# Up-projection of a two-layer trunk on one core: ten panel pairs with a second level of block products instead of eight, and other places for the modulation panels

## The reference, cut to what matters

```python
D_MODEL = 1024; D_FF = 2816; N_MOD = 9
def swiglu(u, w_up, w_down):
    h = u @ w_up                       # 1024 x 5632
    a, b = jnp.split(h, 2, axis=-1)
    return (jax.nn.silu(a) * b) @ w_down

def trunk_layer(l, x, c, ...):
    mod = (jax.nn.silu(c) @ P['ada_w'][l] + P['ada_b'][l]).reshape(B, N_MOD, D)
    sh1, sc1, g1, sh2, sc2, g2, sh3, sc3, g3 = [mod[:, i][:, None, :] for i in range(N_MOD)]
    u = rmsnorm(x, ng[0]) * (1.0 + sc1) + sh1
    x = x + 0.5 * g1 * swiglu(u, P['w_ffn_up'][l, 0], P['w_ffn_down'][l, 0])
    ...                                # token mixing
    u = rmsnorm(x, ng[2]) * (1.0 + sc3) + sh3
    x = x + 0.5 * g3 * swiglu(u, P['w_ffn_up'][l, 1], P['w_ffn_down'][l, 1])
```

## Time and profile before

| | |
|---|---|
| median of three runs | 3149.52 us (3148.24 to 3153.7) |
| the profiled execution | 3147.8 us, span 3146.1 us |
| PE busy | 3096.7 us of the span (98%) |
| DVE, POOL, ACT busy | 1267.5, 1175.2, 417.9 us |
| chain that ended last | PE 95%, DVE 2%, DMA 2%, ACT 1% |
| DMA | 337.64 MB, mean 107 GB/s |
| side panels (ws<-w_ada) | 64 of 1024 KB, median 4.8 us from issue to landing |

### The profile page before, as it was taken

The page is one execution under the profiler, slowest core; times in us unless marked ns, Lnnn a source line. Parts: engine busy times, 40 slices in busy tenths (PEclk is TensorE's granted clock), DMA queues, the critical chain, the costliest instruction groups (busy, mean ns, idle before and its releaser), DMA issues.

```text
span 3146.1 us, 45962 instructions
## 1 busy us (share of the span) xinstructions
PE 3096.7 (98%) x18874; PEld 2502.2 (80%) x18874; DVE 1267.5 (40%) x2645; ACT 417.9 (13%) x806; POOL 1175.2 (37%) x1181
## 2 busy tenths in 40 slices
PE   7999999999999999999999999999999999999999
PEld 5778887678777878888877788876777778788887
DVE  3334532454233464445243344234533234644432
ACT  2000001212111120000011000023021111210000
POOL 4755431210000338764366644302100003487542
PEclk9999999999999999999999999999999999999999
DMA  6564223441111224322225532234311113122221
GB/s 247 196 241 151 86 76 107 155 145 40 52 51 51 85 81 155 114 92 76 86 100 224 217 137 83 80 116 148 125 56 42 44 59 104 67 93 82 85 80 66
DMA packets 73520, 337.64 MB, mean 107 GB/s; under 512 B 10592, under 2 KB 27744, under 8 KB 40288
## 3 DMA queue, kind: packets, MB, share of 16 engines
q1 hardware_dynamic: 63936, 312.03, 27.8%
q0 software_dynamic: 6816, 18.88, 2.0%
q10 hardware_dynamic: 2560, 3.80, 0.3%
HBM read 326.55 MB, written 6.02 MB: 106 GB/s over the span
## 4 chain that ended last, share of the span: by engine, by line
PE 95%; DVE 2%; DMA 2%; ACT 1%; issue 0%; SPq 0%; DVEq 0%; ACTq 0%
PE ps L830 94%; DMA ws<-w_ada 1%; DVE ws L1987 1%; DVE u L1987 0%; DMA lp<-params 0%; ACT ws L1692 0%; DMA ring<-w_ada 0%; ACT u L1692 0%; DVE proj L1987 0%; PE ps L897 0%; DVE masked_room L2415 0%; DVE x L1990 0%; PE ps L1519 0%; DVE masked_room L1987 0%; DVE y L1987 0%
## 5 line engine op out<-in xcount | busy, mean ns | idle before, releaser
L830 PE MATMUL ps<-u,ring 128*128 128x272 f32 x5120 | 1259.7, 397 | 11.5 <-ACT u L1692 9.3
L830 PEld LDWEIGHTS ps<-u,ring 128*128 128x128 f32 x5120 | 950.2, 190 | 231.0 <-issue 27.1
L1987 DVE TENSOR_TENSOR ws<-ws,ps 128x272 f32<-128x272 f32 (+5 forms) x1258 | 497.1, 413 | 1347.2 <-PE ps L830 1331.2
L724 POOL TENSOR_TENSOR masked_room<-ring 128x512 f32<-128x512 f32 (+1 forms) x44 | 55.6, 1265 | 986.7 <-DVE pause L2741 653.3
L1692 ACT ACTIVATE ws<-ps 128x272 f32<-128x272 f32 (+1 forms) x398 | 154.6, 396 | 1260.1 <-PE ps L830 1260.0
L830 PE MATMUL ps<-y,ring 128*128 128x272 f32 (+1 forms) x1376 | 296.7, 353 | 0.0
L830 PE MATMUL ps<-y,ws 128*128 128x272 f32 (+1 forms) x1296 | 296.7, 370 | 0.0
L830 PEld LDWEIGHTS ps<-y,ring 128*128 128x128 f32 x1376 | 230.8, 190 | 50.5 <-issue 10.3
L830 PEld LDWEIGHTS ps<-y,ws 128*128 128x128 f32 x1296 | 227.2, 190 | 35.8
L830 PE MATMUL ps<-proj,ring 128*128 128x272 f32 (+1 forms) x1088 | 240.4, 366 | 1.5 <-DVE proj L1987 1.5
L1692 ACT ACTIVATE ws<-ws 128x272 f32<-128x272 f32 (+4 forms) x170 | 105.8, 633 | 868.7 <-DVE ws L1987 817.2
(11 more groups left out here) (219 smaller groups left out, 3037.2 us busy)
## 6 DMA issues: line engine op xcount, KB each, us to landing
ring<-w_up SPq DMA_DIRECT2D x88, 1024.0 KB, 4.8
ws<-w_ada SPq DMA_DIRECT2D x64, 1024.0 KB, 4.8
ring<-w_down SPq DMA_DIRECT2D x32, 1024.0 KB, 4.8
ring<-w_gate SPq DMA_DIRECT2D x32, 1024.0 KB, 4.8
ring<-w_in SPq DMA_DIRECT2D x22, 1024.0 KB, 4.8
ws<-cache SPq DMA_DIRECT2D x128, 128.0 KB, 3.1
ws<-cache POOLq DMA_DIRECT2D x128, 128.0 KB, 3.4
ring<-w_down SPq DMA_DIRECT2D x16, 768.0 KB, 4.1
```

The costliest lines, as they stand in the source:

```text
L724: nc.gpsimd.tensor_tensor(sums[:, 0], a21, a22, ALU.add).then_inc(w_sums.sem, 1)
L830: return nc.tensor.matmul(out, lhsT, rhs, start=start, stop=stop, skip_group_check=skip)
L1987: return V.tensor_tensor(out, a, b, op)
```

## The change

- `PAIRS` goes from 8 to 10. Panels 2 to 21 are ten pairs, panels 0 and 1 stay single, and the four single panels at the end are gone, with their sums on POOL, additions on DVE and activations on ACT.
- The rooms of the inner token sums move, since `proj` tiles 16 to 19 are now needed for hidden tiles of pairs 8 and 9 while the sums are still read: they lie in `proj` 20 and 21, in the free half of `u`, in a new tile `last_inner`, and one of each four is formed in place in `tsum`.
- The 16 first hidden sums stand elsewhere on DVE: four in pair 8, three in pair 9, eight in pair 10, each time after `c22_b` and before step 4, and the last one after pair 10. They get other rooms (`HID_ROOM`).
- The down-projection's first two sums on POOL wait for pair 10 instead of single panels.
- The modulation panels stand elsewhere within a pair: panel 0 after M2a (before: after M1b), panel 1 after M5a (before: after M2b), panel 2 after the front of 4 (before: after M5b), panel 3 at the pair's end (before: ahead of M3b).

```diff
-PAIRS = 8
+PAIRS = 10
 SINGLE = FT - 2 * PAIRS
...
+HID_ROOM = (8, 9, 10, 11, 12, 13, 14, 4, 5, 6, 7, 0, 1, 2, 3)
...
-        inner_tok = proj[:, 16:22, :].rearrange("p a (b n) -> p (a b) n", n=HALF)
+        last_inner = sb("last_inner", [P, HALF])
...
+        def inner_tok(t, i):
+
+            if i == 2:
+                return tsum[:, t, 0:2, QUARTER:HALF]
+            n = 3 * (t - 1) + (0, 1, None, 2)[i]
+            v = proj[:, 20 + n // 2, HALF * (n % 2):HALF * (n % 2) + HALF] if n < 4 else \
+                u[:, n - 4, HALF:T] if n < 8 else last_inner[:, :]
+            return v.rearrange("p (k n) -> p k n", k=2)
...
                     if r == 1:
-                        inner_token_sums(f, 2)
+                        inner_token_sums(f, 1, True)
+                        inner_token_sums(f, 2, False)
+                        inner_token_sums(f, 2, True)
...
                         plain(3 * a, raw(a, 0, 0), tok(0, 0), True, pr_pe)
-                    side_modulation(l, f, r, 0)
...
                     plain(0, raw(0, 4, 0), tok(4, 0), False, pr_pe)
+                    side_modulation(l, f, r, 0)
                     six[1]()
                     pair_act(pe_, l, f, r, "first_b")
                     plain(3, raw(1, 4, 0), tok(4, 0), False, pr_pe)
-                    side_modulation(l, f, r, 1)
...
                         if a == 0:
+                            side_modulation(l, f, r, 1)
                             seven_[1]()
-                    side_modulation(l, f, r, 2)
...
                     four[0]()
+                    side_modulation(l, f, r, 2)
                     pair_sums(pe_, l, f, r, "S4a")
                     pair_dve(pe_, l, f, r, "c22_a")
                     plain(2, raw(0, 4, 0), tok(4, HALF), False, part)
                     four[1]()
-                    side_modulation(l, f, r, 3)
                     pair_sums(pe_, l, f, r, "S4b")
                     pair_dve(pe_, l, f, r, "c22_b")
                     plain(5, raw(1, 4, 0), tok(4, HALF), False, part)
+                    side_modulation(l, f, r, 3)
...
                     pair_dve(dve, l, n, r, "c22_b")
+                    if r >= PAIRS - 2:
+                        for j0, j1 in (((0, 4),), ((4, 7),), ((7, 11), (11, 15)))[r - PAIRS + 2]:
+                            first_hidden_sums(l, n, j0, j1)
                     step("4", pair_third, pair_third)
...
                     tt_(hid[:, 2 * r:2 * r + 2, HALF:T], halves(pair_gate2), halves(pair_c22), MUL).then_inc(h_done.sem, 2)
+                    if r == PAIRS:
+                        first_hidden_sums(l, n, 15, 16)
```

More of the change, by code:

```diff
@@ L119, in up_product @@
 def up_product(q, name):
[L121 to L124, removed]
+    return {"M1": (1, 2), "M2": (3, 10), "M6": (4, 9), "M7": (5, 11), "M5": (6, 12), "M4": (7, 13),
+            "M3": (8, 14)}[name][q]
 SEG = {0: (0, 0, 512), 1: (1, 0, 384), 2: (2, 0, 256), 3: (1, 384, 128)}
@@ L717, in block_sums @@
                     a11, a12, a21, a22 = w[:, 0:n, 0:P], w[:, n:2 * n, 0:P], w[:, 0:n, P:256], w[:, n:2 * n, P:256]
-                    if stage in ("up0", "up1") and place == 2 + 2 * PAIRS:
+                    if stage in ("down0", "down1") and place == 0:
                         pair_sums(pool, l, int(stage[-1]), PAIRS, "S4b")
-                    elif stage in ("up0", "up1") and place == 3 + 2 * PAIRS:
+                    elif stage in ("down0", "down1") and place == 1:
                         pair_pe(pool, l, int(stage[-1]), PAIRS, "4.3")
@@ L746, in inner_sums, with inner_token_sums @@
                     nc.gpsimd.tensor_tensor(to[3], top[:, 2:4], to[1], ALU.subtract).then_inc(pr_pool.sem, 1)
-                def inner_token_sums(f, t):
+                def inner_token_sums(f, t, in_place):
                     def block(k0, half):
                         return tsum[:, t, k0:k0 + 2, QUARTER * half:QUARTER * half + QUARTER]
-                    rooms = [inner_tok[:, 4 * (t - 1) + i, :].rearrange("p (k n) -> p k n", k=2) for i in range(4)]
+                    rooms = [inner_tok(t, i) for i in range(4)]
                     at = 12 * f + 4 * (t - 1)
[L754 to L760, removed]
+                    if not in_place:
+                        pool.wait_ge(t_sums.sem, t_sums.upto(l, 4 * f + t + 1))
+                        nc.gpsimd.tensor_tensor(rooms[0], block(0, 1), block(0, 0), ALU.subtract).then_inc(in_sums.sem, 1)
+                        pool.wait_ge(in_sums.sem, in_sums.upto(l, at + 1))
+                        nc.gpsimd.tensor_tensor(rooms[1], block(2, 1), rooms[0], ALU.subtract).then_inc(in_sums.sem, 1)
+                        pool.wait_ge(in_sums.sem, in_sums.upto(l, at + 2))
+                        nc.gpsimd.tensor_tensor(rooms[3], block(2, 0), rooms[1], ALU.subtract).then_inc(in_sums.sem, 1)
+                    else:
+                        used = up_product(1, ("M6", "M7", "M4")[t - 1])
+                        pool.wait_ge(t_sums.sem, t_sums.upto(l, 4 * f + 4))
+                        pool.wait_ge(wi_pe.sem, wi_pe.upto(l, 7 * unit_of(f"up{f}", 0) + used))
+                        nc.gpsimd.tensor_tensor(rooms[2], block(2, 1), block(0, 1), ALU.subtract).then_inc(in_sums.sem, 1)
                 def pair_block_sums(f, r):
@@ L795, in weight_sums @@
                 def weight_sums(f):
-                    for q in singles():
+                    for q in range(SINGLE):
                         if f and q == 0:
@@ L1028, in product @@
                     m.then_inc(wi_pe.sem, 1)
[L1030 to L1035, removed]
+                for q in range(SINGLE):
+                    unit, sums_at = f * SINGLE + q, 4 * unit_of(f"up{f}", q)
+                    s = load_number(l, f"up{f}", q) % R
                     sums = wsum[unit_of(f"up{f}", q) % 2]
@@ L1051, in ffn @@
                     if q == 0:
-                        panel(l, f"up{f}", place)
+                        panel(l, f"up{f}", q)
                         product(bx, w(0, 0), tok(0, 0), True, u0=0)
@@ L1090, in ffn @@
                     product(bz, ws_(3), tok(4, HALF), False, frees=True)
+                for r in range(1, PAIRS + 1):
+                    pair(r)
                 seven(l, 2 * f)
@@ L1097, in free_bank @@
                 def free_bank(p, j):
-                    before, last = 7 * p + j - 8, f * SINGLE + SINGLE - 2
+                    before = 7 * p + j - 8
                     if before >= 0:
@@ L1773, in pair @@
                             .then_inc(pr_act.sem, 1)
-                for q in singles():
-                    unit, bx = n * SINGLE + single(q), 3 * (q % 2)
-                    if q == 2 + 2 * PAIRS:
-                        for r in range(1, PAIRS + 1):
-                            pair(r)
+                for q in range(SINGLE):
+                    unit, bx = n * SINGLE + q, 3 * (q % 2)
                     act.wait_ge(wi_pe.sem, wi_pe.upto(l, 7 * unit_of(f"up{n}", 0) + up_product(q, "M1")))
@@ L2209, in pair @@
                     tt_(hid[:, 2 * r:2 * r + 2, HALF:T], halves(pair_gate2), halves(pair_c22), MUL).then_inc(h_done.sem, 2)
-                for q in singles():
-                    if q == 2 + 2 * PAIRS:
-                        for r in range(1, PAIRS + 1):
-                            pair(r)
-                    unit, by, bz = n * SINGLE + single(q), 3 * (q % 2) + 1, 3 * (q % 2) + 2
+                    if r == PAIRS:
+                        first_hidden_sums(l, n, 15, 16)
+                for q in range(SINGLE):
+                    unit, by, bz = n * SINGLE + q, 3 * (q % 2) + 1, 3 * (q % 2) + 2
                     def products(k):
```

53 lines of the change are left out of this document (16 added, 37 removed).

## The result

The changed kernel takes 3156.59 us (median of 20 executions, 3153.41 to 3160.15), the kernel before beside it 3149.44 us (20 executions, 3147.55 to 3155.38). The ratio is 1.0021, with a 95% interval of 1.0014 to 1.0028: 7.1 us slower, where 3156.5 us and 7.0 us were forecast. The profiled execution has a span of 3154.7 us, 8.6 more than before.

What follows compares the result with a forecast made beforehand. PE, busy 98% of the span, was taken to bound the kernel. Against the profiled 3147.8 us, - 10.2 + 19.2 - 2.0 = + 7.0 gave 3154.8; with the runs' median 1.7 us higher, 3156.5, range 3145 to 3164.

Steps and rivals of the forecast that it cites:

- Two pairs for four singles: PE in each of four stages: one pair for two single panels saves 1.27 us, 10.2 us off in all.
- Hidden sums: DVE sums in pairs 8 to 10 and after them make PE late by 4.8 us per stage, 19.2 in all.
- the tail: Last hidden sum, ahead of the down-projection's third product: held up by POOL, PE 1.1 us late per stage.
- Rival 1: DVE's sums are not held up by POOL; only pair 10 costs, 0.5 us per stage; 3139 us, chance 0.15.
- rival 2: Half the lateness of the hidden sums, 2.5 to 3.5 us per stage; 3149 us, chance 0.17.
- Side panels: PE's waits for modulation panel loads, numbered k, with their lower clock: 5.4 instead of 7.7 us, entered as 2 off.
- The narrow places: Shortest distances between side panels, 1 to 2 and 2 to 3: two per pair, waits from 1.8 to about 4.5 us.
- the two long waits shrink by the 2.1 us that 3 to 0 gains: Waits ahead of side panel 1: more room between panels 3 and 0 cuts 2.96 to 0.9 and 1.47 to 0.
- Clock, POOL, loads and rooms: 0: POOL sums, load order and rooms cost nothing; clock priced at zero, at worst 1.5 us in each of four stages.
- rival 3: Stalls also drop the clock and side panels stall at both narrow places: + 16, 3165.5 us, chance 0.10.

Runs made afterwards that it cites:

- run 7: run 4 with the late constants and parameters in up0 loaded with panel 18 instead of panel 12; 3131.89 us, ratio 0.9940 to the kernel before.
- Run 4: Changed kernel with all sixteen hidden sums moved: four at the start of pair 9, seven at the start of pair 10, five behind its c22_b; 3135.07 us, ratio 0.9950.
- run 1: Changed kernel with the seven hidden sums of pairs 8 and 9 taking their second input from PSUM, giving wrong down-projection sums; 3143.34 us, ratio 0.9978.
- run 2: Changed kernel with the seven hidden sums of pairs 8 and 9 moved to the starts of pairs 9 and 10; 3145.35 us, ratio 0.9983.
- run 3: Changed kernel with the sixteenth hidden sum in a free room of y, behind c22_b of pair 10 with the eight others; 3153.88 us, ratio 1.0009.
- run 5: Changed kernel with the side panels back at their old places within a pair; 3162.18 us, ratio 1.0039 to the kernel before.
- run 6: Kernel before, with eight pairs, with only the side panels at the new places; 3145.33 us, ratio 0.9983.

## Why the prediction was right

**Two pairs for four singles: - 10.2.** It holds. Pair 7 takes 24.40 us. In up1 of layer 1, from M3b of pair 7 to the third product of the down-projection, the kernel before takes 3004.43 - 2923.20 = 81.23 us and run 7 takes 78.69, which is the 2.54 us of two pairs for four singles. The third product of the kernel before, and then the two rows of run 7:

```profile
3004.43 3.83 PE L830 MATMUL ps<-ws,masked_room 128*128 128x272 f32 x16
```

```profile
2909.84 5.66 PE L844 MATMUL ps<-u,ring 128*128 128x272 f32 x24
...
2988.53 3.83 PE L844 MATMUL ps<-ws,masked_room 128*128 128x272 f32 x16
```

The times of whole kernels agree. Run 7 has no late sums and 5.5 us less waiting for side panels than before; the half clock behind the 2.96 us wait, 1.5 us, went with it. - 10.2 - 5.5 - 1.5 = - 17.2, measured - 18.7.

**Hidden sums: + 19.2, measured + 20.0 from the rows.** By pair: 2.0 forecast and 2.01 measured, 1.2 and 1.15, 0.5 and 0.70, and for the tail 1.1 and 1.13. Run 4 takes these 20.0 away and is 22.7 us faster. The mechanism was read from a single row, the 2.75 us of two products, and from POOL's times beside it: the two engines take turns by whole instructions. The four sums in 4.34 us and POOL's stretching from 0.72 to 0.92 us show the turns, and run 1 shows that it is the two SBUF inputs. The Trainium skill (SBUF — State Buffer, section "SBUF: two separate sides") counts a VectorE instruction with two SBUF inputs among those that contend with GpSimd while it reads SBUF; by that rule the PSUM form of run 1 should be free, and the trace agrees (1.48 us). Rival 1 (sums not held up, 3139) falls with the gaps of pairs 8 and 9, rival 2 (half the lateness) with their size.

**Side panels: - 2.0, measured - 3.0 to - 5.3.** Right in sign, wrong in size, and the two halves missed in opposite directions. (The prediction's own terms, 7.7 and 5.4 us, differ by 2.3; it entered 2.0.) The narrow places (k = 2 and 3) were to stall for 4.5 us and did so for 0.9. That is one execution: runs 1 to 4 load the side panels at the same places and have 0, 0.8, 1.1 and 2.3 us of such waits, so 4.5 was too much in all five. The changed kernel's three waits, with the granted clock behind the first:

```profile
203.25 1.94 PE L844 MATMUL ps<-ws,csil 128*32 128x256 f32 x16 [2.30 <-DMA ws<-w_ada]
...
1281.38 1.07 PE L844 MATMUL ps<-ws,csil 128*32 128x256 f32 x16 [0.35 <-DMA ws<-w_ada]
...
1663.84 1.07 PE L844 MATMUL ps<-ws,csil 128*32 128x256 f32 x16 [0.58 <-DMA ws<-w_ada]
```

```profile
203.25:207.75 4.50, 4.50 (x31) 3.15 (x32) 0.27 (x1) 0.00 (x0) 4.19 (x5) 0.64 0.30 84
```

The step that failed for k = 1 is "the two long waits shrink by the 2.1 us that 3 to 0 gains". In layer 1 the wait did go. In layer 0 it went only from 2.96 to 2.30 and kept the half clock behind it (0.64 granted, 1.94 us for the x16 row, and 7.81 us from there to side panel 2 instead of 6.28, so about 1.5 us). SP's timeline shows the queue, of the kernel before and then of the changed one (`ws<-w_ada` are the loads of side panels 0 and 1; constants, parameters and two ring panels stand between them):

```profile
183.63 0.33 SPq L644 DMA_DIRECT2D ws<-w_ada  x1
...
190.33 0.33 SPq L644 DMA_DIRECT2D ws<-w_ada  x1
```

```profile
185.13 0.33 SPq L650 DMA_DIRECT2D ws<-w_ada  x1
...
186.45 1.07 SPq L682 DMA_DIRECT2D ring<-w_up  x2
193.90 18.62 SPq L650 DMA_DIRECT2D ws<-w_ada  x3
```

Side panel 1 is issued when panel 0's matmuls end, so its issue and its use move together and stay about 7.1 us apart. What 3 to 0 gained is time for the loads ahead of it: from the issue of panel 0 to that of panel 1 there are now 8.77 us instead of 6.70. But panel 1 landed 18.1 us after panel 0's issue (203.25 - 185.13) where it had landed after 16.9 us (200.51 - 183.63), so 1.2 of the 2.07 us were lost again: it is 9.3 us from issue to landing instead of 10.2, against 7.1 us of cover. I had assumed that the same loads take the same time. For the bulk of the bytes they do: the DMA engines are busy at 376 to 382 GB/s from panel 0's issue for 16.1 us before (to 199.75) and 16.4 after (to 201.50). But then PE goes on 0.8 us later before, and 1.75 us later after; in that time the engines move nothing after the change but a few packets, 33 GB/s from 202.00 to 202.50. Whether these belong to the load, and why PE goes on so late, is open. Run 7 takes the constants and parameters out of the queue, and the wait goes with them. Why the narrow places stall so little was not tried.

**Clock, POOL, loads and rooms: 0.** The other rows of PE's wait table are as before (16.4 and 9.3 us). POOL is busy for 63 us more (1238.2 against 1175.2), and no wait of PE comes from it: the one row that named it was DVE's sum (run 3). The mean granted clock of the 20 executions is 0.9966, that of 27 executions of the kernel before 0.9966 too. So rival 3 falls: gaps of up to 1.8 us, and 16 of them, didn't lower it. The profiled executions differ, however. In 1150 to 1200 us the kernel before, and then the changed one, have

```profile
1150.00:1200.00 50.00, 45.77 (x198) 35.76 (x197) 28.01 (x43) 12.84 (x21) 29.46 (x29) 1.00 0.22 80
```

```profile
1150.00:1200.00 50.00, 46.47 (x188) 36.81 (x187) 26.24 (x45) 12.82 (x21) 26.88 (x26) 0.93 0.18 60
```

that is 50 x 0.07 = 3.5 us of work lost in a stretch that the change doesn't touch. Over all stretches of 50 us it is 10.5 us before and 13.5 after. This is the spread of the executions and no effect of the change.

**The sum.** - 10.2 + 20.0 - 3.0 = + 6.8 against 7.1 measured; in the profiled executions + 3.0 of clock comes on top, 9.8 against 8.6. With the about 5 us of runs 5 and 6 for the side panels it is + 5, inside the interval too (4.4 to 8.8). Whether the side panels are worth 3 or 5 us stays open. That the total was off by 0.1 us is partly luck: sums 0.8 too low, side panels 1.0 to 3.3 too high.

## What to carry to other kernels

Before an instruction is put into a row of work, ask whether its engine idles there, what the other user of SBUF does at that moment, and who waits behind it: the same sixteen sums cost 20 us where the change put them, and nothing when eleven of them stood at the starts of pairs 9 and 10 and five beside an idle POOL. A single odd row in the trace before (two products in 2.75 us where 0.79 is usual) was enough to price the new place within 5%. A load that is issued when its predecessor's use ends gains little when both uses are moved (here 0.66 of 2.07 us); look at what stands ahead of it in the queue.

## What was not expected of the hardware

The granted clock did not follow the length of the wait ahead of it. All but the last of these waits stand at the same place, ahead of side panel 1 in pair 5 of up0 of layer 0, and the clock is the mean of the 4.5 us from the wait's end:

| wait, us | execution | granted clock |
|---|---|---|
| 3.03 | run 5 | 0.62 |
| 2.96 | before | 0.64 |
| 2.42 | run 2 | 0.66 |
| 2.32 | run 1 | 0.62 |
| 2.30 | after | 0.64 |
| 2.43 | run 3 | 1.00 |
| 2.34 | run 4 | 1.00 |
| 2.31 | run 6 | 1.00 |
| 2.32 | run 5, layer 1 | 1.00 |

The rows of run 4 and of run 3 at that place:

```profile
203.63 1.07 PE L844 MATMUL ps<-ws,csil 128*32 128x256 f32 x16 [2.34 <-DMA ws<-w_ada]
```

```profile
204.82 1.07 PE L844 MATMUL ps<-ws,csil 128*32 128x256 f32 x16 [2.43 <-DMA ws<-w_ada]
```

The x16 row takes 1.07 us there and 1.93 or 1.94 in the kernel before and the changed one. So a stall of 2.3 to 2.4 us costs itself and, in some executions, 1.5 us more.
